# Two stages of a tuned trunk kernel re-cut: the rotary step of the attention moved between engines, and the decayed product of the retention split in three passes

## What is computed

```python
q, k, v = jnp.split(h @ w_qkv, 3, axis=-1)
q = rope(rms_norm(q.reshape(B, S, A_HEADS, A_HEAD_DIM), q_gain), pos)
k = rope(rms_norm(k.reshape(B, S, A_HEADS, A_HEAD_DIM), k_gain), pos)
...
s = jnp.einsum('bhnqd,bhnkd->bhnqk', qc, kc) * dmat[None, :, None]
inner = jnp.einsum('bhnqk,bhnkd->bhnqd', s, vc)
...
y = y * lax.rsqrt(jnp.mean(y * y, axis=-1, keepdims=True) + EPS)
return (jax.nn.silu(g) * y) @ w_out
```

## Time and profile before

| what | value |
|---|---|
| median of three runs | 694.58 us (692.86 to 694.67) |
| profiled execution, its own time | 698.26 us |
| span of the profile | 696.0 us |
| TensorE busy (products) | 670.8 us, 96% |
| VectorE busy | 424.6 us, 61% |
| ScalarE busy | 326.9 us, 47% |
| GpSimd busy | 56.5 us, 8% |

### The profile page before, as it was taken

The page is one execution under the profiler, slowest core; times in us unless marked ns, Lnnn a source line. Parts: engine busy times, 40 slices in busy tenths (PEclk is TensorE's granted clock), DMA queues, the critical chain, the costliest instruction groups (busy, mean ns, idle before and its releaser), DMA issues.

```text
span 696.0 us, 8770 instructions
## 1 busy us (share of the span) xinstructions
PE 670.8 (96%) x3281; PEld 558.6 (80%) x3281; DVE 424.6 (61%) x456; ACT 326.9 (47%) x371; POOL 56.5 (8%) x51
## 2 busy tenths in 40 slices
PE   2997999999999999999999999999999999999998
PEld 2875877788888888888888778778888888888886
DVE  2899756677777534447984445535468777753430
ACT  3854565465555333435444554553355555533320
POOL 3396500000000000000000000000000000000000
PEclk9999999999999999999999999999999999999999
DMA  8964244746655555564556454454646665555600
GB/s 289 336 228 146 97 121 121 227 139 191 190 203 184 182 184 196 188 205 135 187 193 223 129 176 139 163 181 140 200 145 190 189 194 191 194 190 182 211 1 30
DMA packets 81468, 121.92 MB, mean 175 GB/s; under 512 B 2032, under 2 KB 43152, under 8 KB 81440
## 3 DMA queue, kind: packets, MB, share of 16 engines
q1 hardware_dynamic: 80736, 119.55, 52.9%
q0 software_dynamic: 496, 1.90, 1.0%
q10 hardware_dynamic: 208, 0.08, 0.0%
HBM read 120.47 MB, written 1.05 MB: 175 GB/s over the span
## 4 chain that ended last, share of the span: by engine, by line
PE 84%; DVE 8%; ACT 3%; issue 2%; DMA 2%; POOL 1%; SPq 0%; DVEq 0%; ACTq 0%
PE acc L462 22%; PE acc L422 16%; PE acc L424 16%; PE acc L423 16%; PE acc L465 11%; DVE lo L860 3%; ACT hi L648 2%; DMA x<-in_x 2%; POOL small L378 1%; PE scr L478 1%; DVE rot L922 1%; DVE small L908 1%; DVE h_both L869 1%; PE scr L595 1%; PE scr L607 0%
## 5 line engine op out<-in xcount | busy, mean ns | idle before, releaser
L860 DVE TENSOR_TENSOR lo<-raw,hi 128x2048 fp32r<-128x2048 f32 x112 | 257.4, 2300 | 139.7 <-ACT hi L648 139.3
L648 ACT ACTIVATE hi<-raw 128x2048 fp32r<-128x2048 f32 x112 | 214.4, 1916 | 133.8 <-PE acc L424 133.8
L462 PE MATMUL acc<-h_both,hi 128*128 128x512 f32 x640 | 226.5, 399 | 0.0
L465 PE MATMUL acc<-h_both,lo 128*128 128x256 f32 x640 | 179.7, 281 | 0.0
L462 PEld LDWEIGHTS acc<-h_both,hi 128*128 128x128 f32 x640 | 120.3, 188 | 29.9
L465 PEld LDWEIGHTS acc<-h_both,lo 128*128 128x128 f32 x640 | 120.9, 189 | 0.0
L422 PE MATMUL acc<-hi,aT_hi 128*128 128x512 f32 x256 | 99.7, 389 | 0.0
L423 PE MATMUL acc<-lo,aT_hi 128*128 128x512 f32 x256 | 99.6, 389 | 0.0
L424 PE MATMUL acc<-hi,aT_lo 128*128 128x512 f32 x256 | 99.6, 389 | 0.0
L422 PE MATMUL acc<-hi,h_both 128*128 128x512 f32 x224 | 92.5, 413 | 0.0
L424 PE MATMUL acc<-hi,h_both 128*128 128x512 f32 x224 | 88.4, 395 | 0.0
(11 more groups left out here) (112 smaller groups left out, 549.4 us busy)
## 6 DMA issues: line engine op xcount, KB each, us to landing
raw<-in_mlp_w SPq DMA_DIRECT2D x64, 1024.0 KB, 5.4
raw<-in_r_w_in SPq DMA_DIRECT2D x24, 1024.0 KB, 5.0
raw<-in_a_w_qkv SPq DMA_DIRECT2D x12, 1024.0 KB, 6.0
raw<-in_r_w_out SPq DMA_DIRECT2D x8, 1024.0 KB, 4.9
raw<-in_a_w_o SPq DMA_DIRECT2D x4, 1024.0 KB, 4.9
x<-in_x SPq DMA_DIRECT2D x2, 512.0 KB, 11.7
out_x<-x SPq DMA_DIRECT2D x4, 256.0 KB, 3.9
decay_sb<-in_decay POOLq DMA_DIRECT2D x1, 768.0 KB, 5.2
```

The costliest lines, as they stand in the source:

```text
L462: nc.tensor.matmul(bank, feat_view(hi, s)[:, kt, o * P:(o + 1) * P], h_both[:, kt, :, :].rearrange("p b t -> p (b t)"), start=kt == 0, sto ...
L465: m = nc.tensor.matmul(bank[:, 0:SEQ], feat_view(lo, s)[:, kt, o * P:(o + 1) * P], hT_hi[:, kt, :], start=False, stop=kt == KD - 1)
L648: nc.scalar.activation(hi[:, s, :], raw[:, s, :], ACT.Copy).then_inc(hi_ready, 1)
L860: nc.vector.tensor_tensor(lo[:, s, :], raw[:, s, :], hi[:, s, :].bitcast(F32), ALU.subtract).then_inc(lo_ready, 1)
```

## The change

In the attention, VectorE now makes the products with cosine and sine itself and reads the finished bank of PSUM for them; the copy `q_raw` is gone. ScalarE squares each head's 128 columns from PSUM with the sum as the instruction's accumulated output, four instructions for a tile. The two adds of the rotated halves are one. GpSimd keeps the power, and multiplies the whole k tile by its factor. The RMS norm's factor is folded into the added constant, so that GpSimd's power gives the final factor at once. The kinds of work stand in other slots and in another order within a slot; "rope" and "raw" come before the variance. Heads 0 to 7 of the attention stand in other slots. VectorE waits for the power before it masks.

In the retention, the decayed scores and the values are each kept in hi and lo (`sT_hi`, `sT_lo`, `v_hi`, `v_lo`), and the product is made in three passes of float32r.

The diff, cut to its core:

```diff
...
-            at[4 * b + 3 + t].append(("raw", p))
-            at[4 * b + 5 + t].append(("rope", p))
-            at[4 * b + 7 + t].append(("T", p))
+            at[4 * b + 3 + t] += [("rope", p), ("raw", p)]
+            at[4 * b + 4 + t].append(("var", p))
+            at[4 * b + 6 + t].append(("T", p))
...
-        if O_AT[h] is not None:
-            at[O_AT[h]].append(("O", h))
-    first_to_last = ["O", "split", "N", "T", "v", "raw", "A", "P", "S", "rope", "E"]
+        at[O_AT[h]].append(("O", h))
+    first_to_last = ["O", "N", "v", "rope", "split", "raw", "var", "T", "A", "P", "S", "E"]
-    at[SLOTS - 1] += [("O", HA - 2), ("O", HA - 1)]
-S_AT = [14, 14, 16, 18, 20, 21, 23, 24]
-P_AT = [16, 17, 18, 20, 23, 24, 25, 26]
-A_AT = [21, 22, 22, 23, 25, 26, 27, 27]
-O_AT = [21, 22, 22, 23, 26, 27, None, None]
+S_AT = [12, 13, 15, 17, 20, 21, 22, 23]
+P_AT = [14, 15, 17, 19, 22, 23, 24, 25]
+A_AT = [20, 21, 21, 22, 24, 25, 26, 26]
+O_AT = [21, 22, 22, 23, 25, 26, 27, 27]
...
+        sT_lo = sb("sT_lo", [P, 384], F32R)
...
-        q_raw = at("q_raw", 40 * KB, [P, 2, 512])
...
-        v_r = at("v_r", 48 * KB, [P, TT, DV])
+        v_hi = at("v_hi", 48 * KB, [P, TT, DV], F32R)
+        v_lo = at("v_lo", 58 * KB, [P, TT, DV], F32R)
+        sT_hi = at("sT_hi", 62 * KB, [P, 384], F32R)
...
+            pool.sem_inc(tables_g_ready, 1)
-                raw4 = q_raw[:, p_i % 2, :].rearrange("p (h d) -> p h d", d=P)
-                cos, sin = [rope_g[:, j % 2, t, part, :].unsqueeze(1).broadcast_to([P, 4, P])
-                            for part in range(2)]
-                pool.wait_ge(raw_qk, 2 * p_i + 1)
-                if p_i >= 2:
-                    pool.wait_ge(rotT_ready, p_i - 1)
-                    pool.wait_ge(rot_ready, p_i - 1)
-                nc.gpsimd.tensor_tensor(rot[:, p_i % 2, :].rearrange("p (h d) -> p h d", d=P),
-                                        raw4, cos, ALU.mult).then_inc(u_ready, 1)
-                nc.gpsimd.tensor_tensor(stage_b[:, p_i % 2, :].rearrange("p (h d) -> p h d", d=P),
-                                        raw4, sin, ALU.mult).then_inc(u_ready, 1)
-                power(small[:, 8 + 4 * (p_i % 2):12 + 4 * (p_i % 2)],
-                      small[:, 4 * (p_i % 2):4 * (p_i % 2) + 4], 4)
+                ss = small[:, 4 * t:4 * t + 4]
+                if j % 2 == 0:
+                    at_q = 24 + 8 * t + 4 * (j // 2)
+                    power(small[:, at_q:at_q + 4], ss, 4)
+                else:
+                    pw = small[:, 8 + 4 * t:12 + 4 * t]
+                    power(pw, ss, 4)
+                    r4 = rot[:, t, :].rearrange("p (h d) -> p h d", d=P)
+                    pool.wait_ge(pow_ready, npow)
+                    pool.wait_ge(rot_sum_ready, p_i + 1)
+                    nc.gpsimd.tensor_tensor(r4, r4, pw.unsqueeze(2).broadcast_to([P, 4, P]),
+                                            ALU.mult).then_inc(k_scaled, 1)
...
-                pe.wait_ge(rot_ready, p_i + 1)
+                if p_i // 2 % 2 == 0:
+                    pe.wait_ge(rot_sum_ready, p_i + 1)
+                else:
+                    pe.wait_ge(k_scaled, 2 * (p_i // 4) + p_i % 2 + 1)
...
-                nc.tensor.matmul(scr[:, 1, :], sT[:, 0:P], v_r[:, 0, :],
-                                 start=True, stop=True).then_inc(y_ready, 1)
-                nc.tensor.matmul(scr[:, 2, :], sT[:, P:SEQ], v_r[:, 0, :], start=True, stop=False)
-                nc.tensor.matmul(scr[:, 2, :], sT[:, SEQ:384], v_r[:, 1, :],
-                                 start=False, stop=True).then_inc(y_ready, 1)
+                def decayed(dst, columns, t, first_term, last_term):
+                    return three(dst, sT_hi[:, columns], sT_lo[:, columns], v_hi[:, t, :], v_lo[:, t, :],
+                                 first_term, last_term)
+                decayed(scr[:, 1, :], slice(0, P), 0, True, True).then_inc(y_ready, 1)
+                decayed(scr[:, 2, :], slice(P, SEQ), 0, True, False)
+                decayed(scr[:, 2, :], slice(SEQ, 384), 1, False, True).then_inc(y_ready, 1)
...
-            def raw_copy(p_i):
+            def head_squares(p_i):
-                if t == 0:
-                    act.wait_ge(tok0_ready, j + 1)
+                act.wait_ge(rope_read, p_i + 1)
+                if p_i == 0:
+                    act.wait_ge(ssq_ready, 4)
-                    act.wait_ge(used, 2 * j + 2 + RING)
-                bank = acc[:, p_i % 4, :]
+                    act.wait_ge(squares_qk, 4 * p_i)
-                    act.wait_ge(rot_ready, p_i - 1)
-                nc.scalar.copy(q_raw[:, p_i % 2, :], bank).then_inc(raw_qk, 1)
-                nc.scalar.activation(stage_a[:, p_i % 2, :], bank, ACT.Square).then_inc(raw_qk, 1)
+                    act.wait_ge(pow_ready, p_i)
+                for h in range(4):
+                    nc.scalar.activation(junk[:, h * P:(h + 1) * P], acc[:, p_i % 4, h * P:(h + 1) * P],
+                                         ACT.Square, accum_out=small[:, 4 * t + h:4 * t + h + 1]
+                                         ).then_inc(squares_qk, 1)
...
-                        raw_copy(i)
+                        head_squares(i)
...
-                    nc.scalar.activation(v_r[:, t, :], acc[:, t, :], ACT.Copy,
-                                         scale=nrm[:, 2, t:t + 1]).then_inc(v_r_ready, 1)
+                    nc.scalar.activation(v_hi[:, t, :], acc[:, t, :], ACT.Copy,
+                                         scale=nrm[:, 2, t:t + 1]).then_inc(v_hi_ready, 1)
+                act.wait_ge(sT_full_ready, h + 1)
+                nc.scalar.activation(sT_hi[:], sT[:], ACT.Copy).then_inc(sT_hi_ready, 1)
...
-                own(nc.vector.tensor_scalar(nrm[:, 3, :], nrm[:, 2, :], 1.0 / P, None, ALU.mult))
...
-            def head_variance(p_i):
-                t = p_i % 2
-                ss = small[:, 4 * (p_i % 2):4 * (p_i % 2) + 4]
-                dve.wait_ge(raw_qk, 2 * p_i + 2)
-                dve.sem_inc(acc_free, 1)
-                own(nc.vector.reduce_sum(ss, stage_a[:, p_i % 2, :].rearrange("p (h d) -> p h d", d=P),
-                                         axis=AX))
-                nc.vector.tensor_scalar(ss, ss, nrm[:, 3, t:t + 1], EPS, ALU.mult,
-                                        ALU.add).then_inc(var_ready, 1)
+            own(nc.vector.tensor_scalar(nrm[:, 5, :], nrm[:, 0, :], EPS, None, ALU.mult))
+            own(nc.vector.tensor_scalar(nrm[:, 6, :], nrm[:, 0, :], EPS * P, None, ALU.mult))
+            dve.wait_ge(tables_g_ready, 1)
-                u4 = stage_b[:, p_i % 2, :].rearrange("p (h d) -> p h d", d=P)
-                r4 = rot[:, p_i % 2, :].rearrange("p (h d) -> p h d", d=P)
-                pw = small[:, 8 + 4 * (p_i % 2):12 + 4 * (p_i % 2)]
-                dve.wait_ge(u_ready, 2 * p_i + 2)
-                for o in range(2):
-                    a, b = slice(o * 64, o * 64 + 64), slice((1 - o) * 64, (1 - o) * 64 + 64)
-                    dv.mark(nc.vector.tensor_tensor(r4[:, :, a], r4[:, :, a], u4[:, :, b], ALU.add))
-                power_done()
+                raw4 = acc[:, p_i % 4, :].rearrange("p (h d) -> p h d", d=P)
+                cos, sin = [rope_g[:, j % 2, t, part, :].unsqueeze(1).broadcast_to([P, 4, P])
+                            for part in range(2)]
+                u4 = stage_b[:, t, :].rearrange("p (h d) -> p h d", d=P)
+                r4 = rot[:, t, :].rearrange("p (h d) -> p h d", d=P)
+                if t == 0:
+                    dve.wait_ge(tok0_ready, j + 1)
+                else:
+                    dve.wait_ge(used, 2 * j + 2 + RING)
+                if p_i >= 2:
+                    dve.wait_ge(rotT_ready, p_i - 1)
+                sin_done = dv.mark(nc.vector.tensor_tensor(u4, raw4, sin, ALU.mult))
+                nc.vector.tensor_tensor(r4, raw4, cos, ALU.mult).then_inc(rope_read, 1)
+                dve.wait_ge(dv.sem, sin_done)
+                dve.wait_ge(rope_read, p_i + 1)
+                ur = stage_b[:, t, :].rearrange("p (h o d) -> p h o d", o=2, d=64)[:, :, ::-1, :]
+                rr = rot[:, t, :].rearrange("p (h o d) -> p h o d", o=2, d=64)
+                nc.vector.tensor_tensor(rr, rr, ur, ALU.add).then_inc(rot_sum_ready, 1)
+            def head_variance(p_i):
+                j, t = p_i // 2, p_i % 2
+                ss = small[:, 4 * t:4 * t + 4]
+                dve.wait_ge(squares_qk, 4 * p_i + 4)
+                dve.sem_inc(acc_free, 1)
-                    heads = slice(24 + 8 * t + 4 * (j // 2), 28 + 8 * t + 4 * (j // 2))
-                    dve.wait_ge(dv.sem, dv.now())
-                    nc.vector.tensor_scalar(small[:, heads], pw, nrm[:, 1, t:t + 1],
-                                            float(P) ** -0.5, ALU.mult,
-                                            ALU.mult).then_inc(rot_ready, 1)
+                    i = nc.vector.tensor_scalar(ss, ss, nrm[:, 6, t:t + 1], None, ALU.add)
```

(32 more changed lines are left out.)

## The result

The changed kernel takes 689.18 us (median of six runs, 687.75 to 690.31), the kernel before in the same comparison 694.62 us. The ratio is 0.9918, with a 95% interval of 0.9901 to 0.9934: 5.4 us or 0.82% faster, where 2.5 us were forecast. The time lies at the lower edge of the range; the size of the gain is off by a factor of two.

A forecast was written before the change was run, and what follows sets the result against it. TensorE, busy 96% of the span, was taken as the bound: its work and waits. Retention 2.1 plus attention 0.4 made 2.5 us less than 698.26, 695.8; off the median, 692.1 us, range 689.0 to 695.7.

The forecast's parts named there:

- Retention: Retention product: nine float32r products replace three float32 ones, 0.52 us less a head, 2.1 us for four; new VectorE/ScalarE work hidden.
- the forecast's lower bound: Retention: gain of only 1.8 us if each of three product groups also pays some 0.03 us for its start.
- the sum 9.65 against 10.1: Attention: TensorE's waits plus slow clock lose 9.65 us after the change against 10.1 before, a gain of 0.4 us.
- The walk: Attention: the new order followed by half-steps; TensorE waits 3.3 us at tile 2, half-step 28 starts at 123.3.
- The waits: Attention: TensorE's waits after the change, 3.3, 0.9, 1.35, 0.7, 1.3 and 0.4 us.
- The slow stretch of the clock: Attention: TensorE's lower clock expected again behind the first k tile's wait, costing 1.7 us.
- The base: Whole kernel: 2.5 us taken off the profiled execution's 698.26 us, the same sum off the median giving 692.1.
- 0.28: Whole kernel: the part of the likeliest case's 0.43 (691 to 693.5 us) counted as faster, below 692.5.
- The prices: Attention: rope tile done 2.0 us after its start, four ScalarE squares 1.15, GpSimd's k tile multiplication 1.3.
- The first, a k tile in time: Attention rival: first k tile's wait 1.5 us, no slow stretch; 1.8 + 1.7 go, 688.6 to 690.5 us; chance 0.25.
- The second, an attention that gives back the retention's gain: Attention rival: six waits with squares nearer 1.9 us add 2 to 3 us; 693.5 to 696.5 us; chance 0.20.
- The slower one: Attention rival: squares of 2.0 us make k tiles chain up, 6.2 us more, 698.3 us; chance 0.12.

The follow-up runs named there:

- e5: The changed kernel, unchanged, run again beside the kernel before on one chip; 688.83 us, ratio 0.9914 to the kernel before.
- e10: The changed kernel, unchanged, a third time, on the same chip as the variance-first kernel; 688.71 us, ratio 0.9910 to the kernel before.
- e1: The kernel before with only the retention's product in three passes; ratio 0.9957 to the kernel before, 3.0 us.
- e2: The changed kernel with the old retention product, so the attention's change alone; ratio 0.9941 to the kernel before, 4.1 us.
- e4: The changed kernel with a tile's variance before the split within a slot; 686.49 us, ratio 0.9859 to the kernel before.
- e9: The changed kernel with the variance before the split, run again beside the unchanged changed kernel; 685.17 us, ratio 0.9857 to the kernel before.
- e6: The variance-first kernel with A of head 2 and O of head 3 both in slot 22; ratio 0.9868 to the kernel before.

## Why the prediction was off

**Retention: right.** Forecast 2.1 us, measured 2.2 in the stage from the first decayed product to the second MLP, in the changed kernel and alone. A start of 0.03 us for each group, which the forecast's lower bound supposed, shows nowhere: the nine products take 2.04 us. (By that supposition the bound would be 1.7 us and not 1.8; nothing hangs on it.) The new work on VectorE and ScalarE is hidden as written: `sT_lo` is done at 398.5, the split behind it starts at 399.38, and TensorE never waits in that stage.

**Attention: the step that failed is the sum 9.65 against 10.1, a gain of 0.4 us.** The mechanism was right to the place: the first k tile's variance stands behind one split and GpSimd's multiplication behind the next. The walk had that multiplication done at 52.75 and TensorE asking at 49.5; it was done at 51.96 and asked for at 49.0, so the wait was 3.0 instead of 3.3 us. Half-step 28 started at 121.26, forecast at 123.3. Three terms were mis-sized or missing, and a fourth, smaller one has no name.

*The waits.* 7.95 us were forecast, and the profiles show 6.8 (changed kernel), 6.3 (`e5`) and 7.2 (`e10`), against 8.4 before. One of the forecast waits, 0.9 us for the probabilities of head 1, never was: the table puts N one slot behind S, so in slot 14, ahead of the split that I put it behind. The output projection's wait was 0.9 instead of 1.3, that for the values 0.2 instead of 0.4; tile 6's was 1.8 instead of 1.35. On the mean of the three, 6.8, this is worth 1.2 us.

*The slow stretch of the clock.* I charged 1.7 us in every execution. All three profiles in which the attention is the old one (the two of the kernel before and `e1`) have it, behind a wait of 3.1 us each time. Of the changed attention with its orders untouched, it is in two profiles (waits of 3.0 and 3.4) and not in two (`e5` and `e2`, 2.6 each). The mean granted clock, which is on record for every execution, says how often it comes: 0.998 or 0.997 in the profiles that have one such stretch, 0.999 or 1.000 in those that have none. So counted, 8 of the 18 executions of the changed kernel have one and 10 none; of 44 of the kernel before, 27 have one, 9 none, and 8, at 0.995, are taken for two. By this count, an estimate, the kernel before loses 1.7 us on average and the changed kernel 0.75, so 0.9 us more of gain.

*Outside the span.* The kernel's own time exceeds its span by 2.2 to 2.4 us wherever the attention is the old one, and by 1.7 to 1.9 us wherever it is the new one, `e1` and `e2` included. On the means, 2.28 and 1.80, that is 0.5 us, which no step had. What does it was not tried.

*A rest of 0.3 us.* From the first product to the first MLP the three profiles of the changed kernel take 2.7, 4.2 and 2.6 us less than before. The listed waits give 1.6, 2.1 and 1.2 of it, the slow stretch 1.7 in `e5`, and TensorE's earlier change to the fast pace at the start (last section) about 0.75, 0.05 and 1.1. Each time some 0.3 us is left that no listed wait holds.

What the runs show comes together as: retention 2.2, waits 8.4 - 6.8 = 1.6, slow stretch 0.9, outside the span 0.5, the rest 0.3, 5.5 us in all, against 5.4 measured, and 6.0 and 6.3 by the ratios of the two later comparisons. The intervals of the three, 4.6 to 6.9, 4.0 to 8.0 and 4.4 to 8.2 us, hold the sum; how often the slow pace of the MLPs comes is not in it.

**The base.** The prediction counted from one execution of 698.26 us and took the difference over to the median. Since differences were carried over, the slow-paced MLP stretches did it no harm; a reader who had compared the two spans would have found 8.1 us of gain, 3.4 of them not the change's. The chances carry a slip of a hundredth: 0.28 and the first rival's 0.25 make 0.53 for faster, and slower was 0.12.

**The prices** held: rope 2.0 us, the four squares 1.0 from the first one's start to the next instruction's against 1.15, the multiplication alone 1.04 against 1.3. By the errata table of the Trainium skill, VectorE: DVE Perf Modes, one square is estimated at 0.25 us; the duration was 0.27 to 0.33 and the pace with the read 0.25 to 0.27, so page and rows differ by nothing that counts. The rule in the Trainium skill, SBUF — State Buffer, on the shared pair held in both directions: GpSimd's multiplication took 2.43 us behind a split of VectorE's and 1.04 without one, and in `e4` VectorE's add of two SBUF operands (52.37) took 1.22 instead of 0.69 us while GpSimd multiplied (52.00 to 53.04), and sine and cosine, with one operand in PSUM, kept 0.68 at the same place in the changed kernel (53.39, with GpSimd busy from 53.00).

**The rivals.** The first, a k tile in time, is what `e4` makes true by one move in a list. It gives 3.5 us beside the changed kernel (`e9`, `e10`), the number of the sum for it (1.8 + 1.7), but of other terms: the waits fall by 2.7 us, from 6.8 to 4.1, and the slow stretch gives 0.75, as it was in 8 of 18 executions only. That the two sums agree is luck. The second, an attention that gives back the retention's gain, fell with the waits, which came out smaller and not larger. The slower one needed squares at 2.0 us; they took 1.0.

## What to carry to other kernels

When a chain crosses engines, look for what each of its short operations stands behind in its queue: here a 0.2 us variance behind a 2.3 us split cost 3.5 us, and the cure was the order of two words. A wait on TensorE has two prices, itself and the slow stretch that may follow: it followed the waits of 2.9 us and more in six profiles, at 1.7 us each, and none of the waits of 2.6 in two. And before two spans are compared, profile the same kernel twice and compare its untouched stages.

## What was not expected of the hardware

The same products on an unhindered TensorE at full granted clock take 88.83 us in one MLP and 90.53 us in another, in the same program; in `e2`, `e6` and `e10` both within one execution, in the kernel before the slow pace twice in one execution and the fast one twice in another. Of the 24 such stretches in the twelve profiles, five are slow. What sets it is open.

The start of the kernel has a hand in what happens at 50 us. After the long wait for its first operands TensorE's products are 0.43 us apart, until they fall to 0.23. In the changed kernel's profile this comes 2.2 us after the first product, on the timeline of TensorE:

```profile
16.87 0.77 PE L427 MATMUL acc<-hi,h_both 128*128 128x512 f32 x1
...
18.72 0.48 PE L428 MATMUL acc<-lo,h_both 128*128 128x512 f32 x1
19.04 0.40 PE L429 MATMUL acc<-hi,h_both 128*128 128x512 f32 x1
19.27 0.40 PE L427 MATMUL acc<-hi,h_both 128*128 128x512 f32 x1
```

In `e5` it comes 3.5 us after the first product, in `e10` 1.4, in the kernel before 3.5. TensorE then reaches the k tile earlier or later, while the tile is ready 35.1 to 35.2 us after the first product in all three: waits of 2.6 (`e5`), 3.0 and 3.4 us (`e10`), and behind the longer two the lower clock. Most of what was gained at the start was lost again there, and with the slow stretch 1.5 us more on balance: from the first product to the output projection the three take 88.1, 89.5 and 89.6 us.
